# Two stacked blocks on one core: the weight's high half times both halves of the operand as one 512-column product, and first keys of 16 columns

## What is computed

```
def second_block(x, mem, positions, ...):
    h = x
    for i in range(DEPTH):                                   # DEPTH = 2
        if i % 2 == 0:
            h = h + even_mixer(h, positions, ...)            # latent attention, recurrent mixer
        else:
            h = h + mamba2_mixer(h, ...)                     # state-space mixer
        h = h + memory_cross_attention(h, mem, ...)          # 4 heads of 128, 256 memory rows
        h = h + swiglu_ffn(h, ffn_norm[i], ffn_w13[i], ffn_w2[i])   # 1024 -> 2 x 2816 -> 1024

# hgrn2, per chunk: a[q, k] = sum_d q[q, d] k[k, d] exp(cb[q, d] - cb[k, d]) for k <= q, then a @ v
```

## Time and profile before

| | before |
|---|---|
| median of 3 runs | 2472.75 us (2469.75 to 2476.2) |
| profiled execution, its own time | 2473.57 us |
| its span, first to last instruction | 2471.8 us |
| mean granted TensorE clock | 0.994 |
| TensorE (PE) busy, matmuls | 97%, 20238 |
| DVE, ACT, POOL busy | 56%, 55%, 81% |

### The profile page before, as it was taken

The page is one execution under the profiler, slowest core; times in us unless marked ns, Lnnn a source line. Parts: engine busy times, 40 slices in busy tenths (PEclk is TensorE's granted clock), DMA queues, the critical chain, the costliest instruction groups (busy, mean ns, idle before and its releaser), DMA issues.

```text
span 2471.8 us, 51427 instructions
## 1 busy us (share of the span) xinstructions
PE 2385.9 (97%) x20238; PEld 2295.4 (93%) x20238; DVE 1376.0 (56%) x2489; ACT 1352.6 (55%) x2347; POOL 1995.8 (81%) x2171
## 2 busy tenths in 40 slices
PE   9999999999999999999999999989899999999999
PEld 8999999999999989999999999788899998898999
DVE  7784432557726865433558544654546347864650
ACT  5545556556645545556457655562554446656553
POOL 8987668899989977779899988241469998686998
PEclk9999999999999999999999999999999999999999
DMA  7554444456655544445456765120246665343665
GB/s 210 148 145 118 140 128 145 135 163 177 182 169 158 148 137 138 128 132 157 137 166 196 227 170 154 43 86 20 62 132 192 190 177 154 95 135 105 187 190 161
DMA packets 692382, 360.79 MB, mean 146 GB/s; under 512 B 13776, under 2 KB 689968, under 8 KB 692144
## 3 DMA queue, kind: packets, MB, share of 16 engines
q1 hardware_dynamic: 689168, 350.15, 49.4%
q10 hardware_dynamic: 2976, 7.36, 1.0%
HBM read 349.72 MB, written 1.05 MB: 142 GB/s over the span
## 4 chain that ended last, share of the span: by engine, by line
PE 69%; DVE 12%; POOL 10%; ACT 5%; issue 3%; DMA 2%; SPq 0%; ACTq 0%; DVEq 0%; POOLq 0%
PE pb L281 68%; POOL wl L372 10%; ACT wh L359 1%; ACT pool L309 1%; DVE bx L3644 1%; PE pb L586 1%; DVE pool L3825 1%; DVE u2l L682 0%; DVE pool L3683 0%; DMA raw<-in_ffn_w 0%; DVE pool L1044 0%; DMA raw<-in_w_ffn_in 0%; DVE bx L692 0%; ACT pool L310 0%; ACT bx L309 0%
## 5 line engine op out<-in xcount | busy, mean ns | idle before, releaser
L372 POOL TENSOR_TENSOR wl<-raw,wh 128x256 fp32r<-128x256 f32 (+1 forms) x2164 | 1990.1, 951 | 463.2 <-ACT wh L359 442.2
L359 ACT ACTIVATE wh<-raw 128x1024 fp32r<-128x1024 f32 (+2 forms) x669 | 690.5, 1034 | 458.6 <-PE pb L281 240.2
L281 PE MATMUL pb<-xh,wh 128*128 128x272 f32 (+2 forms) x3104 | 923.0, 297 | 13.5 <-POOL wl L372 2.2
L281 PE MATMUL pb<-xh,wl 128*128 128x272 f32 (+2 forms) x3104 | 885.4, 285 | 0.0
L281 PE MATMUL pb<-xl,wh 128*128 128x272 f32 (+2 forms) x3104 | 885.1, 285 | 0.0
L281 PEld LDWEIGHTS pb<-xh,wh 128*128 128x128 f32 x3104 | 586.5, 189 | 35.4 <-issue 12.5
L281 PEld LDWEIGHTS pb<-xl,wh 128*128 128x128 f32 x3104 | 586.7, 189 | 2.2
L281 PEld LDWEIGHTS pb<-xh,wl 128*128 128x128 f32 x3104 | 586.1, 189 | 0.0
L281 PE MATMUL pb<-pool 64*64 64x64 f32 (+11 forms) x2944 | 234.7, 257 | 24.5 <-DVE pool L1192 2.7
L281 PE MATMUL pb<-u2h,wh 128*128 128x256 f32 x840 | 239.1, 285 | 2.6 <-DVE u2l L682 2.6
L281 PE MATMUL pb<-u2l,wh 128*128 128x256 f32 x840 | 234.4, 279 | 0.0
(11 more groups left out here) (422 smaller groups left out, 3681.8 us busy)
## 6 DMA issues: line engine op xcount, KB each, us to landing
raw<-in_w_in SPq DMA_DIRECT2D x208, 512.0 KB, 3.9
raw<-in_ffn_w SPq DMA_DIRECT2D x120, 512.0 KB, 4.0
raw<-in_w_ffn_in SPq DMA_DIRECT2D x88, 512.0 KB, 3.8
raw<-in_w_branch SPq DMA_DIRECT2D x48, 512.0 KB, 3.6
raw<-in_od_w_in SPq DMA_DIRECT2D x41, 512.0 KB, 3.8
raw<-in_w_ffn_out SPq DMA_DIRECT2D x32, 512.0 KB, 3.8
raw<-in_ev_w_in SPq DMA_DIRECT2D x20, 512.0 KB, 3.9
raw<-in_w_out SPq DMA_DIRECT2D x16, 512.0 KB, 3.6
```

What stands on the lines that cost most here:

```text
L281: return e.matmul(out, lhsT=l, rhs=r, start=a, stop=z, skip_group_check=True)
L359: E.e.activation(hi, src, ACT.Copy).then_inc(*sig("weight_hi", ("hi", g)))
L372: E.e.tensor_tensor(lo[:, s, :], src[:, s, :], hi[:, s, :].bitcast(F32), SUB).then_inc(*sig("weight_lo", *[("lo", g, i) for i in ks]))
```

## The change

Two edits. First, in the second block, a projection is *folded* if it has 256 columns, its operand is x, u2 or hid, and its kind is not one of the two of the state-space mixer's inner projections. High and low part of an operand become two halves of one tensor (XHL, U2HL, HIDHL). For a folded tile `paired` issues two matmuls for a block instead of three: high weight x [high | low] with 512 columns into the whole bank, and low weight x high with 256 into its first half. At the tile's end ACT copies the second half of the bank into a buffer `stage` of 128 x 256 (`a_half`), and DVE adds that to the first half in place (`v_fold`); what takes the tile out now waits for this fold instead of the last matmul. There is one `stage`, so a copy also waits for the fold before it.

Second, the first keys' products of hgrn have weights of 16 columns instead of 128 and write 16 rows of the bank; they stand behind the near products of their level, with their wait for the last level's first keys.

```
+    def folded(p):
+        return p.n == NS and p.x in ("x", "u2", "hid") and p.kind not in ("xbc", "zg")
+    def done_at(p, g):
+        return at("fold", g) if folded(p) else at("mm", g)
+    def v_fold(E, p, j, r, g):
+        b = banks[place(p, j, r)]
+        E.e.wait_ge(*at("half", g))
+        E.e.tensor_tensor(b[:, 0:NS], b[:, 0:NS], STAGE[:, :], ADD).then_inc(*sig("out_v", ("fold", g)))
+    def a_half(E, p, j, r, g):
+        E.e.wait_ge(*at("mm", g))
+        if E.staged is not None:
+            E.e.wait_ge(*at("fold", E.staged))
+        E.e.activation(STAGE[:, :], banks[place(p, j, r)][:, NS:2 * NS], ACT.Copy).then_inc(*sig("out_a", ("half", g)))
+        E.staged = g
...
     def pe_project(E, p):
-                o = banks[place(p, p.js[mi], r)][:, p.t0:p.n]
+                o = banks[place(p, p.js[mi], r)][:, p.t0:2 * NS if folded(p) else p.n]
...
-                    m = three(E, g, o, xh, xl, k, kk == 0, kk == p.KT - 1)
+                    m = (paired(E, g, o, both_halves(p.x, kk), k, kk == 0, kk == p.KT - 1) if folded(p) else
+                         three(E, g, o, xh, xl, k, kk == 0, kk == p.KT - 1))
...
     def v_project(E, p):
                     E.settle()
+                    if folded(p):
+                        v_fold(E, p, p.js[mi], r, g)
                     if p.kind in V_EVAC:
...
     def a_project(E, p):
                     E.settle()
+                    if folded(p):
+                        a_half(E, p, p.js[mi], r, g)
                     if p.kind in A_EVAC:
...
     def v_res(E, p, j, r, g):
         x = p.aux["add"][:, j, 0:p.n]
-        E.e.wait_ge(*at("mm", g))
+        E.e.wait_ge(*done_at(p, g))
...
     def pe_hgrn(E, li):
-            if lv in HG_FIRST:
-                if lv != 9:
-                    e.wait_ge(*at("hg_at", li, n - 1, 0))
-                elif half:
-                    e.wait_ge(*at("hg_at", li, 4, 0))
-                for hd in range(4):
-                    m = mm(e, banks[3][:, hd * NM:hd * NM + NM], L[:, hd, 0:P], R[:, hd, 0:NM], True, True)
-                m.then_inc(*sig("hg_scores", ("hg_scores", li, n, 0)))
             if lv in HG_NEAR or lv == 6:
...
+            if lv in HG_FIRST:
+                if lv != 9:
+                    e.wait_ge(*at("hg_at", li, n - 1, 0))
+                elif half:
+                    e.wait_ge(*at("hg_at", li, 4, 0))
+                for hd in range(4):
+                    m = mm(e, banks[3][0:NM, hd * NM:hd * NM + NM], L[:, hd, 0:NM], R[:, hd, 0:NM], True, True)
+                m.then_inc(*sig("hg_scores", ("hg_scores", li, n, 0), ("hg_sc", li, n)))
...
+    def paired(E, g, o, x, k, first, end):
+        hi, lo = WH[g % NHL], WL[g % NHL]
+        c = slice(k * P, (k + 1) * P)
+        mm(E.e, o.rearrange("p (a t) -> p a t", a=2), hi[:, c], x, first, end)
+        return mm(E.e, o[:, 0:NS], lo[:, c], x[:, 0, :], False, end)
```

More of the change, by code:

```diff
@@ L211, in program @@
     WL = [sb(f"wl{i}", [P, 1024], F32R) for i in range(NHL)]
-    with nc.sbuf_tensor("xh", [P, 8, NT], F32R) as XH, nc.sbuf_tensor("xl", [P, 8, NT], F32R) as XL:
+    with nc.sbuf_tensor("xhl", [P, 2, 8, NT], F32R) as XHL:
         pass
+    XH, XL = XHL[:, 0], XHL[:, 1]
     XF = sb("xf", [P, 2 * 8 * NT])
@@ L234, in program @@
         pass
+    with nc.sbuf_tensor("topool", [P, PW], F32), nc.sbuf_tensor("stage", [P, NS], F32) as STAGE:
+        pass
     with nc.sbuf_tensor("to8704", [P, 8704], F32), nc.sbuf_tensor("dh0", [P, 1, NT], F32R) as DH0:
@@ L243, in program @@
         pass
-    with nc.sbuf_tensor("to14336", [P, 14336], F32), nc.sbuf_tensor("u2h", [P, 8, NS], F32R) as U2H, \
-            nc.sbuf_tensor("u2l", [P, 8, NS], F32R) as U2L:
+    with nc.sbuf_tensor("to14336", [P, 14336], F32), nc.sbuf_tensor("u2hl", [P, 2, 8, NS], F32R) as U2HL:
         pass
-    with nc.sbuf_tensor("hidh", [P, 22, NT], F32R) as HIDH, nc.sbuf_tensor("hidl", [P, 22, NT], F32R) as HIDL:
+    with nc.sbuf_tensor("hidhl", [P, 2, 22, NT], F32R) as HIDHL:
         pass
+    U2H, U2L, HIDH, HIDL = U2HL[:, 0], U2HL[:, 1], HIDHL[:, 0], HIDHL[:, 1]
     with nc.sbuf_tensor("to8192", [P, 8192], F32), nc.sbuf_tensor("sgh", [P, 8, NS], F32R) as SGH:
@@ L388, in operand, with both_halves @@
         return hi[:, p.t0:], lo[:, p.t0:]
+    def folded(p):
+        return p.n == NS and p.x in ("x", "u2", "hid") and p.kind not in ("xbc", "zg")
+    def both_halves(x, k):
+        return {"hid": HIDHL, "u2": U2HL}.get(x, XHL)[:, :, k, 0:NS]
+    def done_at(p, g):
[10 more added lines that the diff above has]
+        E.staged = g
     def whole(p, k):
@@ L620, in v_rope_tile @@
         E.nrope += 1
-        e.wait_ge(*at("mm", g))
+        e.wait_ge(*done_at(p, g))
         if p.name == "dq0" and j == 0:
@@ L2494, in pe_x_early @@
             for k in range(3):
-                three(E, g, banks[r % 3][:, 0:NS], XH[:, k, 0:NS], XL[:, k, 0:NS], k, k == 0, False)
+                paired(E, g, banks[r % 3][:, :], both_halves("x", k), k, k == 0, False)
+    def paired(E, g, o, x, k, first, end):
[3 more added lines that the diff above has]
+        return mm(E.e, o[:, 0:NS], lo[:, c], x[:, 0, :], False, end)
     def three(E, g, o, xh, xl, k, first, end):
@@ L3984, in walk @@
     def walk(E):
-        E.sums = False
+        E.sums, E.staged = False, None
         E.do("begin")
```

12 lines of the change are left out of this document (6 added, 6 removed).

## The result

The changed kernel takes 2516.52 us (median of 4 runs, 2515.5 to 2518.08) where the kernel before took 2471.26 beside it. The ratio is 1.017, 95% interval 1.0147 to 1.0193 (the two medians alone give 1.018). That is 45 us slower, and outside the range of the prediction (2458 to 2487), whose forecast was 2476.5. The profiled execution took 2515.5 us, its span is 2513.7.

What follows compares the result with a forecast made beforehand. TensorE, busy 97% of the span, was taken as the bound. Terms -9.9 + 11.0 + 3.2 + 2.4 + 2.5 + 2.0 - 7.5 = +3.7 us on the profiled 2473.6, 0.8 over the runs' median, gave 2476.5; range 2458 to 2487.

Steps and rivals of the forecast that it cites:

- The merged product: Folded projections: one 512-column matmul replaces two of 256, saving 8 ns a step over 1240 counted steps, -9.9 us.
- The rival of a column a cycle: Merged matmul: 512 columns take 0.213 us, saving 22 ns a step, total 2459 to 2467 us; chance 0.17.
- the rival that nothing is saved: Merged matmul: 512 columns take 0.235 us, so the 9.9 us fall away, total 2486 us; chance 0.14.
- Output projections of cross attention: Two stages of eight tiles: ACT leads at 2.45 us a tile, TensorE resumes 5.5 us later in each, +11.0 us.
- The queries' tiles: Cross attention's query tiles: first tile 0.84 us later, next one's lateness half uncovered, 1.2 us each, +2.4 in all.
- The first mixer's output: First mixer's output projection: ACT takes 2.88 us a tile where residuals were 2.84 apart, +3.2 us.
- Memory keys and values: 16 tiles sharing DVE and ACT with the recurrent mixer: copies delay other ACT work, +2.0 us, between 0 and 6.
- Latents and recurrent projections: Before the memory stage: merged steps save -0.9 us with TensorE setting the pace; a third of a latency costs +0.3.
- First keys: hgrn levels: eight first-key passes shrink from 0.89 to 0.37 us, saving 5.2 in second halves, 2.3 in first, -7.5 us.
- The rival that DVE and ACT pace the levels: hgrn: ACT's exponentials and DVE's products pace the levels, so first keys bring nothing, total 2484 us; chance 0.11.
- the prediction's own sign of being wrong there: hgrn's first halves: a TensorE wait that grows by as much as the passes shrink.
- The granted clock: TensorE's clock level: read as 1.00 or near it in all windows before the change, no cost forecast.

Runs made afterwards that it cites:

- E4: Changed kernel with folds only in the two gated FFNs and their output projections, first-key change kept: 2469.22 us, 0.9991 of the kernel before.
- E5: Changed kernel with ACT's weight split for three pieces ahead placed behind a folded tile's copy instead of ahead of it: 2501.51 us.
- E6: Changed kernel, but tiles going into the residual have no copy or fold; DVE adds both bank halves to the residual: 2492.85 us.
- E9: Changed kernel without memory folds, but DVE alone waits there for every memory tile's last matmul, doing no work: 2511.81 us.
- E3: Changed kernel without memory folds, but ACT and DVE both wait there for every tile's last matmul, doing no work: 2515.43 us.
- E1: Changed kernel with no tile folded, three matmuls a step; only the first-key change remains: 2474.0 us, 1.0003 of the kernel before.
- E7: Changed kernel with the fold's copy moved from ACT to DVE, so copy and add are both on DVE: 2495.41 us.
- E2: Changed kernel with the 16 tiles of the memory keys and values not folded: 2510.01 us, 1.014 of the kernel before.
- E12: Kernel before plus 16-column first keys at their old place, FFN outputs folded with two adds, gated FFNs with copy and add on DVE: 2467.82 us.

## Why the prediction was wrong

By its steps:

- *The merged product:* right in kind, a term mis-sized. 512 columns took 0.229 us (forecast 0.227), but a step saves 4 ns, not 8, and the -9.9 us were about -3: the FFN stages give 2.7 (3.9 in E4), and the rest is lost in stages that TensorE no longer paces. The rival of a column a cycle is out, the rival that nothing is saved nearly came true for this term.
- *Output projections of cross attention:* right in kind and size, +6.0 in the first against 5.5. E5 and E6 show that it is ACT's order, as argued. Around them I missed some 5 us a stage. The queries' tiles (forecast +1.2) do not show: the two waits of the earlier trace rows are 4.0 us instead of 3.9. One to 2 us lie at the FFN's start (E4), which the prediction had at nothing.
- *The first mixer's output:* +7.2 instead of +3.2. The mechanism was right, and two adds in E6 take 6.0 of it away; ACT's tile took 2.99 us, not 2.88, and the milestone takes in part of the next stage's start. The granted clock of 0.90 instead of 1.00 is in the 7.2 as well.
- *Memory keys and values:* **the step that failed.** "Between 0 and 16 x 0.4 = 6 I take +2.0, since those waits are mostly for other chains." It was +12.1. I priced only the latency that a copy adds to ACT's list. But DVE now stands in line for every tile, where it stood for every second one before, and the chains I called other run over DVE: E9 shows 5.7 us from DVE's waits alone. The other 6.5 or so go with the work of copies and adds (E3 against the changed kernel), and whether through their time or through ACT's and DVE's rounds was not tried apart.
- *Latents and recurrent projections:* forecast -0.9 + 0.3, measured +5.5. I had let TensorE set the pace there. ACT and DVE do, once a tile goes out at 2.7 us instead of 1.5 and a backlog is not worked off any more. In this stage that is read from the trace (three tiles from 1498.7 to 1504.1 in ACT, 1497.7 to 1500.7 in E1). E5, where only ACT's order differs, takes 3.4 of the 5.5 away, as far as its milestones can be compared; E7, with DVE doing the copy, takes none away.
- *First keys:* size of the passes right (0.36 against 0.37), -7.5 was -2.5. The rival that DVE and ACT pace the levels is true for the first halves, where TensorE's waits for DVE grew from 2.7 to 8.3 us and all waits together by 5.6, the prediction's own sign of being wrong there. It was given 0.11.
- *The granted clock:* a term at nothing. "The granted clock is 1.00 or near it in all of them" is true of the kernel before (0.97 from 1485 to 1700), but the prediction took it for granted after the change too. It fell to 0.90 to 0.95 in the stages where TensorE came to wait, and at most some 14 of the 42 us go with it; they are spread over the terms above.

Sum of what was measured: -2.5 + 0.3 + 5.5 + 12.1 + 7.2 + 11.0 - 0.7 - 0.4 + 11.0 - 2.0, in the order of the table, and 0.7 at the end make 42.

## What to carry to other kernels

When work moves from one engine to a hand-over between two others, write out one tile's round through their lists, with every wait that stands in line, and compare it with the tile's time on the engine that is relieved. A copy on one engine that another must answer before the first goes on (0.36 us of work) cost 0.95 us of standing still a tile; the same two adds without the hand-over (E6) leave the three output stages 1.2 to 2.4 us longer than before, instead of 7.2 to 11.0. A wait that is brought into TensorE's way can cost more than its own length, since the granted clock was lower near such waits here. And an in-order engine that must now wait for each tile, not every second, delays all that is behind it in its list, however idle it is on average.

## What the runs showed that was not expected

One stretch of the first block, which no kernel here changes, took 8 to 14 us longer in some executions (E2, E5 and E12 in the table). In each of the three TensorE waited there 7.1 us for DVE. The timeline of DVE has two adds there; in E2:

```profile
1158.55 10.76 DVE L1895 TENSOR_TENSOR xhl<-pool,xhl 128x1088 fp32r<-128x1088 f32 x2 [0.77 <-ACT xhl L1889]
```

and in E1:

```profile
1160.02 3.06 DVE L1895 TENSOR_TENSOR xhl<-pool,xhl 128x1088 fp32r<-128x1088 f32 x2 [0.76 <-ACT xhl L1889]
```

One add of 1088 columns, both operands in the state buffer, took 9.56 us in E2 (9.57 in E5 and E12), where E1's four of this line take 1.3 to 3.0. POOL's weight differences ran alongside, in E2 without a break from 1154.50 until 1166.97, 1.1 us before that add ended:

```profile
1154.50 12.47 POOL L375 TENSOR_TENSOR wl<-raw,wh 128x256 fp32r<-128x256 f32 x18
```

In E1 POOL ran through the adds as well, and there the first of them took 1.31:

```profile
1154.59 15.50 POOL L375 TENSOR_TENSOR wl<-raw,wh 128x256 fp32r<-128x256 f32 x19
```

The Trainium skill (page "SBUF — State Buffer", section "SBUF: two separate sides") has a DVE instruction with two operands in SBUF and one of GpSimd share a pair of ports, which the first to start holds for its whole length while the other is blocked. The rows of E2 fit that in part: the add ended about its own usual time after POOL's run did, but it was held up by a dozen of POOL's instructions (0.7 us each) and not by one. Why DVE came through in E1 and not in E2 was not tried. Such a difference of 8 to 14 us in unchanged code is why stages were compared rather than medians.
